# Store wait moved off a phase barrier, recurrence steps reordered, and a pair of attention turns shifted, in a hybrid attention and recurrence layer on one core

## The reference

```python
def hybrid_layer(x, c_act, positions, lb, ...):
    shift, scale, gate = split(c_act @ w_ada + b_ada)
    h = rms_norm(x, norm_w) * (1 + scale) + shift
    aq, ak, av, ag, rq, rf, ri, rg = split(h @ w_in)      # 1024 x 6656 weights
    # A: 16 query heads, 4 key heads of 64, window 128, a sink logit per head
    aq, ak = rope(rms_norm(aq)), rope(rms_norm(ak))
    attn = sliding_window_attention(aq, ak, av, sinks) * silu(ag)
    # B: gated linear recurrence, 8 heads of 128, in chunks of 64
    f = lb + (1 - lb) * sigmoid(rf)
    rec = rms_norm(hgrn2_chunkwise(rq, f, ri)) * silu(rg)
    return x + gate * (concat([attn, rec]) @ w_out)

def hgrn2_chunkwise(q, f, i):                  # per chunk of 64 tokens
    b = cumsum(log f);  q_dec = q * exp(b);  k_inv = (1 - f) * exp(-b)
    a = tril(q_dec @ k_inv.T)
    o = a @ i + q_dec @ state
    state = exp(b_last) * state + k_out.T @ i
```

## Time and profile before

| | before |
|---|---|
| device time, median of 3 | 1800.18 us (1797.7 to 1800.46) |
| device time of the profiled execution | 1800.81 us |
| its span | 1799.0 us |
| PE busy | 1762.8 us, 98% |
| DVE busy | 1284.7 us, 71% |
| ACT busy | 975.7 us, 54% |
| POOL busy | 476.0 us, 26% |
| mean granted TensorE clock | 0.995 |

### The profile page before, as it was taken

The page is one execution under the profiler, slowest core; times in us unless marked ns, Lnnn a source line. Parts: engine busy times, 40 slices in busy tenths (PEclk is TensorE's granted clock), DMA queues, the critical chain, the costliest instruction groups (busy, mean ns, idle before and its releaser), DMA issues.

```text
span 1799.0 us, 28392 instructions
## 1 busy us (share of the span) xinstructions
PE 1762.8 (98%) x9856; PEld 1507.0 (84%) x9856; DVE 1284.7 (71%) x2628; ACT 975.7 (54%) x2127; POOL 476.0 (26%) x825
## 2 busy tenths in 40 slices
PE   6999999999999999999999999999999999999998
PEld 4788888999978888878888889998888888888887
DVE  7965466777767666697646577776776667987986
ACT  5622224888876565652222488888655565343441
POOL 1000025777722122200002477773222220000000
PEclk9999999999999999999999999999999999999999
DMA  9242332222123444344133322131433158178252
GB/s 362 70 164 88 123 105 101 75 71 77 51 83 104 124 139 134 105 168 164 69 128 108 110 69 75 39 95 38 179 95 100 54 161 320 70 257 296 102 176 94
DMA packets 158494, 222.30 MB, mean 124 GB/s; under 512 B 11792, under 2 KB 104336, under 8 KB 150672
## 3 DMA queue, kind: packets, MB, share of 16 engines
q1 hardware_dynamic: 158352, 220.49, 36.2%
HBM read 163.18 MB, written 57.28 MB: 123 GB/s over the span
## 4 chain that ended last, share of the span: by engine, by line
PE 89%; DVE 4%; issue 2%; ACT 2%; POOL 2%; DMA 1%; SPq 0%; POOLq 0%; ACTq 0%; DVEq 0%
PE bank L918 70%; PE bank L1108 3%; PE bank L1094 3%; PE bank L1078 3%; PE bank L1183 2%; PE bank L1203 1%; PE bank L1218 1%; PE bank L1179 1%; PE bank L1029 1%; PE bank L1231 1%; PE bank L1208 1%; DVE g_lo L1916 1%; PE bank L893 0%; ACT sm L1545 0%; POOL q_rinv L2607 0%
## 5 line engine op out<-in xcount | busy, mean ns | idle before, releaser
L918 PE MATMUL bank<-h_hi,w_hi 128*128 128x512 f32 x512 | 207.1, 405 | 0.2
L918 PE MATMUL bank<-h_lo,w_hi 128*128 128x512 f32 x512 | 200.4, 391 | 0.0
L918 PE MATMUL bank<-h_hi,w_lo 128*128 128x512 f32 x512 | 200.1, 391 | 0.0
L918 PE MATMUL bank<-wq_hi,h_hi 128*128 128x384 f32 x512 | 179.6, 351 | 0.5 <-issue 0.5
L918 PE MATMUL bank<-ob_hi,oa_hi 128*128 128x512 f32 x448 | 175.0, 391 | 0.2 <-DVE ob_lo L2357 0.2
L918 PE MATMUL bank<-ob_hi,oa_lo 128*128 128x512 f32 x448 | 174.4, 389 | 0.0
L918 PE MATMUL bank<-ob_lo,oa_hi 128*128 128x512 f32 x448 | 174.3, 389 | 0.0
L918 PE MATMUL bank<-wq_hi,h_lo 128*128 128x384 f32 x512 | 172.1, 336 | 0.0
L918 PE MATMUL bank<-wq_lo,h_hi 128*128 128x384 f32 x512 | 171.4, 335 | 0.0
L1399 ACT ACTIVATE g_hi<-g_raw 128x2048 fp32r<-128x2048 f32 x36 | 68.9, 1914 | 162.5 <-PE bank L918 156.4
L1545 ACT ACTIVATE sm<-sm,neg_m 128x257 f32<-128x257 f32 x256 | 127.6, 501 | 6.6 <-DVE neg_m L2163 1.4
(11 more groups left out here) (256 smaller groups left out, 4670.2 us busy)
## 6 DMA issues: line engine op xcount, KB each, us to landing
g_raw<-in_w_in SPq DMA_DIRECT2D x24, 1024.0 KB, 6.0
raw<-in_w_in SPq DMA_DIRECT2D x16, 1024.0 KB, 8.3
o_lower<-mixed_cols SPq DMA_DIRECT2D x32, 512.0 KB, 6.4
nat_rows<-u SPq DMA_DIRECT2D x48, 256.0 KB, 2.6
raw<-in_w_in SPq DMA_DIRECT2D x8, 1536.0 KB, 6.7
o_upper<-in_w_out SPq DMA_DIRECT2D x24, 512.0 KB, 8.8
wa<-in_w_ada SPq DMA_DIRECT2D x8, 1024.0 KB, 10.9
g_q<-gate_cols SPq DMA_DIRECT2D x64, 128.0 KB, 2.9
```

The costliest lines, as they stand in the source:

```text
L918: mm = pe.matmul(dst, a, b, start=(first and m == 0), stop=(last and m == 2), **more)
```

## The change

It has these parts.

1. The wait for the attention's last stores moves from SP's end of the attention to SP's step t = 2 of the recurrence, and a wait of the same kind is added on ACT in front of step 1's `decays`.
2. In a recurrence step `chunk_products` is split. The turn of the keys (`chunk_turn`) stands ahead of the outputs, the scores (`chunk_scores`) behind them, and `mix_transposes` moves from the front of the step to behind the projection of the queries. Turned rows go to bank 5 in all steps. ACT copies them (`mix_copy`) one step later, and SP stores them one step later (`spill(t - 4)`), which leaves quads 14 and 15 for behind the loop.
3. At step 16 of segment 0 `gemm_p1(1, 0, 1)` moves to the front of the step; `last_quads` is reordered likewise; the waits of `out_part` and of the dense stage on banks follow the new banks.
4. In the attention, `turn_qk` of pair 2 moves from the pair's start into its first projection, as pair 1 has it.
5. The low-part conversions of the next weights on DVE are spread over two places of a pair (`next_weights(s, m, slot)`), at step 16 DVE's `weights_t1` goes behind the masked scores, and the `carry` of keys on SP comes one block earlier.

```diff
             # SP, end of attention
                 if s + 1 < SEGS:
                     sp.wait_ge(carry_out, 48 * GROUPS)
-                for i in range(2):
-                    sp.wait_ge(att_out[i], (s + 1) * 16 * (ATT_B // 2))
             # SP, recurrence
                 for t in range(REC_T + 2):
+                    if t == 2:
+                        for i in range(2):
+                            sp.wait_ge(att_out[i], (s + 1) * 16 * (ATT_B // 2))
...
-                    if t >= 3:
-                        spill(t - 3)
+                    if t >= 4:
+                        spill(t - 4)
                 sp.wait_ge(rmix_ok, QB * (base + REC_T))
                 if s + 1 < SEGS:
                     load_quarter(GU * (s + 1), B22)
...
-                spill(REC_T - 1)
+                for t in range(REC_T - 2, REC_T):
+                    spill(t)
             # PE, attention
-                if 2 <= m <= PAIRS:
+                if 3 <= m <= PAIRS:
                     turn_qk(s, j)
                 if m < PAIRS:
                     project_block(s, 2 * m, range(KH))
-                    if m == 1:
+                    if 1 <= m <= 2:
                         turn_qk(s, j)
             # PE, recurrence step
-                    if t >= 3:
+                    if t == REC_T:
+                        gemm_p1(s + 1, 0, 1)
+                    if t == REC_T + 1:
                         mix_transposes(s, t - 3)
+                    if 1 <= t <= REC_T:
+                        chunk_turn(T - 1, t - 1)
                     if t >= 2:
                         outputs(T - 2, t - 2)
                     if 2 <= t <= REC_T:
-                        chunk_products(s, T - 1, t - 1)
+                        chunk_scores(s, T - 1, t - 1)
...
                         project_q(s, h, j)
                     if t == 1:
-                        chunk_products(s, T - 1, t - 1)
-                    if t == REC_T and s + 1 < SEGS:
-                        gemm_p1(s + 1, 0, 1)
+                        chunk_scores(s, T - 1, t - 1)
+                    if 3 <= t <= REC_T:
+                        mix_transposes(s, t - 3)
                     if 1 <= t <= REC_T:
                         chunk_states(s, T - 1, t - 1)
             # PE, last_quads
-                mix_transposes(SEGS - 1, t - 3)
                 out_part(0, 0, 0, 0)
                 out_part(0, 0, 0, 1)
-                chunk_products(SEGS - 1, T - 1, t - 1)
+                chunk_turn(T - 1, t - 1)
                 outputs(T - 2, t - 2)
+                chunk_scores(SEGS - 1, T - 1, t - 1)
                 out_part(0, 0, 1, 0)
+                mix_transposes(SEGS - 1, t - 3)
                 chunk_states(SEGS - 1, T - 1, t - 1)
             # ACT
             def decays(s, t):
+                if t == 1:
+                    for i in range(2):
+                        act.wait_ge(att_out[i], (s + 1) * 16 * (ATT_B // 2))
                 act.wait_ge(midsum_ok, T + 1)
...
-                    if t >= 3 and not (s + 1 == SEGS and t == REC_T):
+                    if 4 <= t <= REC_T:
+                        mix_copy(s, t - 4)
+                    if t > REC_T:
+                        mix_copy(s, t - 3)
             # DVE
-                    if s + 1 < SEGS and t == REC_T:
-                        weights_t1(GU * (s + 1))
                     if 1 <= t <= REC_T:
                         ... # masked scores a_T
+                    if s + 1 < SEGS and t == REC_T:
+                        weights_t1(GU * (s + 1))
```

More of the change, by code:

```diff
@@ L1185, in outputs, with chunk_turn, chunk_scores @@
                 mm.then_inc(o_ok, 1)
-            def chunk_products(s, T, t):
+            def chunk_turn(T, t):
+                b = t % 2
+                pe.wait_ge(kinv_ok, T + 1)
+                geq(pe, knat_ok, T)
+                for q in range(QB):
+                    mm = pe.transpose(bank[3][:, tokens(q)], k_inv[b][:, tokens(q)], ident[:])
+                mm.then_inc(k_turned, 1)
+            def chunk_scores(s, T, t):
                 b = t % 2
@@ L1739, in recurrence @@
                         hi_a11(s + 1)
-                    if t >= 2 and not (s + 1 < SEGS and t >= REC_T):
+                    if 2 <= t < REC_T or (s + 1 == SEGS and t > REC_T):
                         mix_squares(s, t)
@@ L2220, in mix_block, with next_weights @@
                                          ALU.mult, ALU.mult).then_inc(omix_ok, 1)
[L2222 removed]
+            def next_weights(s, m, slot):
                 g, at = m // (NBLK // 2), m % (NBLK // 2)
[L2225 to L2226 removed]
+                part = ((None, None), (None if g == 0 else 0, None), (0, 1) if g == 0 else (1, None), (2, 3))[at][slot]
+                if m < PAIRS and g + 1 < GROUPS:
+                    if part is not None:
                         att_weights_lo(s, g + 1, part)
[L2228 removed]
+                elif m < PAIRS and 1 <= at <= 2 and slot == 0:
                     rec_weights_lo(s, 0, (at - 1,))
@@ L2267, in att_pair @@
                     sum_squares(s, 2 * m + 1)
+                next_weights(s, m, 1)
                 if m == PAIRS:
```

46 lines of the change are left out of this document (13 added, 33 removed).

## The result

The changed kernel took 1810.87 us (median of 4 runs, 1809.11 to 1812.39) against 1799.65 us before (median of 4): a ratio of 1.0059, with a 95% interval of 1.0047 to 1.0072. That is 11 us slower; 1809.0 had been forecast. The profiled execution, the fastest of the four, took 1809.11 us with a span of 1807.3 us, 8.3 us above the span before.

The account below looks back on a forecast made before the run. PE was taken as the bound, busy 1762.8 of 1799.0 us. Terms -2.2 + 0.2 + 1.8 + 3.4 + 0 + 3.9 + 1.7 = +8.8; 1800.8 + 8.8 - 0.6 = 1809.0 us, range 1799.5 to 1813.

Parts of the forecast that it names:

- the carry: Attention, SP's transfers of keys and values one block earlier: lies beside PE's work, 0.
- Stores at the seam: Quad 14's store, issued behind the 1 MB load, delays ACT's `s_hi[S1]` and the product: +3.9, plus +1.7 for a spell.
- Rival A: At the seam quad 14's store lands early, near 791.2, beside the load's packets: +3.6, 1803.8 us; chance 0.13.
- Pair 2: Attention, both segments: late turns shift ACT's chain, two gaps become one of about 2.3: +0.9 each, +3.4 for two spells.
- B: No spells in the attention: merged gap stays under the threshold, or ACT's chain shifts by less: +5.4, 1805.6 us; chance 0.15.
- D: ACT's chain at pair 2 has slack, both gaps go: 1795.8 us with an early store, 1801.0 with a late one; chance 0.13.
- Barrier: Segment 0, early recurrence: `k_nat` ready in time, L1183 1.75 earlier, key turn's 0.44 no longer behind it: -2.2.
- Segment 1's same place: No barrier wait shows there: table load behind the wait +0.65, key turn moved ahead -0.44: +0.2, no spell.
- Seam, 0: Front of step 16: dense group covers PE's 2.42 wait, given back at quad 14's row turn and the states: 0.
- Spread conversions: DVE's low-part weight conversions in two places of an attention pair: lie beside PE's work, 0.
- Steady steps: Recurrence steps: PE does the same matmuls in another order, its own projection hiding the new waits: 0.
- Last steps: End of the recurrence: the gap of 0.61 ends with DVE's state chain, which starts from the same projection: 0.

Follow-up runs that it names:

- turns behind 6 matmuls: Pair 2's turns behind 6 matmuls of the projection, against the kernel with store, turns and conversions put back and ACT's wait ahead of the table load: 1798.11 us.
- the best version: The change with store, turns, conversions and `weights_t1` put back and ACT's wait moved ahead of the table load: 1796.27 us; with the barrier's wait put back instead, 1796.49.
- the early wait: ACT's wait for the attention's stores moved ahead of the table load, on the changed kernel with store, turns and conversions put back: 1798.84 us.

## Why the prediction was right

The time, the sign and the two mechanisms that carry the sum were right. The prices of nothing for the carry, the spread conversions, segment 1's steps and the last steps were not, and the forecast came as close as it did in part by luck: 1.1 too little at the stores and 0.8 at the end stand against nearly 1 too much for the spells at pair 2.

*Stores at the seam, +3.9 and +1.7.* The step was right, the spell measured +1.71, and the size was 1.1 short: it measured +5.03. I had the row of `o_last` landing at 795.2, 0.7 behind the load, and took 794.7 instead. In the changed kernel the store again lands 0.7 behind the load, and the load, which waits for DVE's finished rows, is itself issued 0.4 later relative to the product before and takes 0.2 longer. Rival A, a store that gets through early, was not seen in any of the four kernels with this order: it took 6.4 us in the changed kernel, 6.0 with the turns and 7.2 with the barrier's wait put back, and 6.9 in the kernel before with the part alone.

*Pair 2, +0.9 and a spell in each segment.* It measured +0.83 and +0.76, and a spell both times. Rivals B and D fall: ACT's chain has no slack, as the turns behind 6 matmuls show once more. But of the 1.7 us for each spell 1.2 and 1.3 were left at the end of the attention. What made up for the rest was not traced.

*Barrier, -2.2.* From the scores to L1183 the gain was 1.71, where 1.75 had been forecast, and the next wait was the one named, the state chain, with a gap of 1.29 and no spell. The key turn's 0.44 behind it can't be told apart in the next stretch (-0.12 for -0.44). What the forecast missed is that the change takes away the wait for `k_nat` twice. The moved wait alone does it (11.99 to 10.29 us), and the carry alone does it better (to 9.63), since it puts nothing in front of the table load. With both in the kernel, the moved wait only costs: putting it back made the place 0.66 earlier. I had read the 2.9 us for which SP waited for the last store and not asked why that store was issued so late; three transfers stood ahead of it, and I had priced their move at nothing.

*Segment 1's same place, +0.2.* At L1187 +0.73 where +0.65 had been forecast; with the wait moved ahead of the table load, or taken out, it is gone. The table load behind the wait is real. The trace shows it without a drain, as read: in the run with the conversions put back `to_mid` starts at 1264.15, straight behind a load of 1.28 from 1262.86.

*Seam, 0.* It measured -0.12, and PE gave back the 2.42 at the row turn of quad 14, where a gap of 1.99 with a spell stands now, as forecast. But "the same work in another order" on DVE was not free: with one DVE operation put back the product came 1.97 earlier, of which 0.9 was left at the product from S1.

*Spread conversions, 0.* Right beside the late turns, wrong by itself: 0.6 in each segment as soon as PE was on time.

*Steady steps, 0.* Right for segment 0, 0.6 too little for segment 1.

*Last steps, 0.* It measured +0.8, a gap of 0.67 at 1540.35, in front of which DVE waited for a load of `o_lower`. I looked for the late store of quad 14 as its cause, and the runs don't bear that out: with the store put back the gap was 0.24 in one, under 0.1 in three, and 0.40 to 1.03 in three others, and the load's arrival at DVE, counted from the last quads' L1187, varied from 21.9 to 23.1 us among them. None of the four kernels with the old order of steps has the gap. What moves it is open.

## What to carry to other kernels

When a step is delayed in a hand-written order, follow what is left behind the loop on the queue that issues transfers: one 256 KB store that slips behind a 1 MB load turns 2.3 us into 6.4, and whoever reuses its memory pays that. Where a barrier waits for a transfer, ask first what was issued ahead of it; moving three small transfers made the kernel 2.7 us faster, where moving the wait left its time the same. A price of nothing holds only with the cover that stands there now, so undo the large loss and look again: the conversions' 1.2 us came into sight only then. And when a change has many parts, try the small ones alone on the kernel before: here one changed number had most of the gain of the best version.

## What the runs showed of the hardware that I had not expected

Whether a gap of PE is followed by a half-clock spell is not settled by its length alone. The state gap at the seam was 2.42 before and had a spell; with the part of the store alone in the kernel before, the same gap (2.36 at 768.01) had none. The gap for the row turn of quad 14 is 1.99 or 2.00 in eight kernels, six times with a spell behind it and twice without. The windows, first of the kernel with the store's part alone, then of the one with the store and the turns put back, and of the one with the early wait:

```profile
768.00:774.00 6.00, 5.99 (x41) 1.00 1.01 386
```

```profile
773.00:779.00 6.00, 4.10 (x27) 1.00 0.21 79
```

```profile
773.00:779.00 6.00, 5.27 (x26) 0.72 0.14 52
```

No gap of up to 1.4 us had one of its own here, the gaps of 2.2 to 2.3 at pair 2 had one each time (six in three kernels), and between 1.7 and 2.4 both were seen (those of 2.6 and 2.7 and those of 3.65 to 5.42 at the seam all had one). The gap of 1.7 at 51 us, untouched by any of this, had one in 6 of the 14 traces, and explains a part of the 3 to 6 us by which runs of one kernel differ. Nor is the price always 1.7: over the 6 us from 774.00, behind the gap of 2.00 in the kernel with the conversions put back, the granted clock was 0.51, and over those from 799.00 in the kernel before with the store's part alone it was 0.60, so up to 2.9 and 2.4 us were lost. So a gap near 2 us should be priced with a chance, not a sum, and medians of several runs are needed to tell 2 us.
